# Columns turned half a chunk later, and one modulation shared by ScalarE and POOL, at the entry of the second attention layer

## The reference

```python
shift, scale, gate = jnp.split(silu_c @ w_ada[i] + b_ada[i], 3, axis=-1)
u = h * (1.0 + scale[:, None, :]) + shift[:, None, :]
uc = hc * (1.0 + scale_c) + shift_c
if i % N_MIXERS == 0:
    y, yc = mixer_a(u, uc, ...)      # windowed attention
else:
    y, yc = mixer_b(u, uc, ...)      # 2-D neighbourhood attention
h = layer_norm_2(DEEPNORM_ALPHA * h + gate[:, None, :] * y, ln_g[i], ln_b[i])
```

## Time and profile before

| | |
|---|---|
| median of three runs | 2012.42 us (2010.51 to 2013.0) |
| the profiled execution's own time | 2013.87 us |
| its span | 2012.0 us |
| TensorE busy | 1960.5 us, 97% |
| VectorE busy | 1052.8 us, 52% |
| ScalarE busy | 802.6 us, 40% |
| POOL busy | 725.9 us, 36% |
| mean granted clock of TensorE | 0.992 of 2.4 GHz |

### The profile page before, as it was taken

How to read it: one execution, slowest core, us unless ns; L and a number is a source line. 1 busy time by engine, 2 the same in 40 slices (tenths; PEclk the granted TensorE clock), 3 DMA queues, 4 the chain that set the end, 5 groups by cost and what they waited for, 6 DMA issues and landing times.

```text
span 2012.0 us, 36191 instructions
## 1 busy us (share of the span) xinstructions
PE 1960.5 (97%) x14644; PEld 1627.4 (81%) x14644; DVE 1052.8 (52%) x2196; ACT 802.6 (40%) x1568; POOL 725.9 (36%) x559
## 2 busy tenths in 40 slices
PE   7999999999999999999999999999999999999996
PEld 5888888888887888888888788778888888888785
DVE  4556655865856554556665732733333333334625
ACT  3110110110125565566767620645454454555601
POOL 3333333333345822221222524562232232232545
PEclk9999999999999999999999999999999999999998
DMA  4423322232232401100111423131111111111333
GB/s 160 136 84 95 107 93 81 98 114 74 84 105 85 154 16 36 46 22 25 35 36 35 135 79 116 53 126 43 46 40 43 49 37 43 50 35 43 111 121 136
DMA packets 51044, 152.24 MB, mean 76 GB/s; under 512 B 5440, under 2 KB 11200, under 8 KB 50752
## 3 DMA queue, kind: packets, MB, share of 16 engines
q1 hardware_dynamic: 50160, 148.73, 22.3%
q10 hardware_dynamic: 720, 1.20, 0.2%
HBM read 129.20 MB, written 20.71 MB: 75 GB/s over the span
## 4 chain that ended last, share of the span: by engine, by line
PE 65%; DVE 3%; ACT 2%; issue 2%; POOL 1%; DMA 0%; DVEq 0%; SPq 0%; POOLq 0%
PE psum L935 16%; PE psum L936 15%; PE psum L937 15%; PE psum L1123 7%; PE psum L1071 6%; PE psum L1087 5%; PE psum L944 1%; POOL w_lo L758 0%; ACT u_tmp L1335 0%; DMA w_raw<-weights_in 0%; ACT u_hi L1336 0%; DVE logits L1848 0%; ACT logits L1411 0%; DVE prob_t L1870 0%; DVE u_lo L1715 0%
## 5 line engine op out<-in xcount | busy, mean ns | idle before, releaser
L935 PE MATMUL psum<-u_hi,w_hi 128*128 128x512 f32 (+1 forms) x1440 | 545.8, 379 | 3.0 <-DVE u_lo L1715 2.1
L936 PE MATMUL psum<-u_lo,w_hi 128*128 128x512 f32 (+1 forms) x1440 | 527.3, 366 | 0.0
L937 PE MATMUL psum<-u_hi,w_lo 128*128 128x512 f32 (+1 forms) x1440 | 526.7, 366 | 0.0
L756 POOL CAST w_hi<-w_raw 128x1024 fp32r<-128x1024 f32 x140 | 152.9, 1092 | 992.6 <-DMA w_raw<-weights_in 992.6
L758 POOL TENSOR_TENSOR w_lo<-w_raw,w_hi 128x1024 fp32r<-128x1024 f32 x140 | 348.0, 2486 | 11.2
L935 PEld LDWEIGHTS psum<-u_hi,w_hi 128*128 128x128 f32 x1440 | 272.6, 189 | 57.1 <-DVE u_lo L1715 3.7
L937 PEld LDWEIGHTS psum<-u_hi,w_lo 128*128 128x128 f32 x1440 | 272.8, 189 | 46.2
L936 PEld LDWEIGHTS psum<-u_lo,w_hi 128*128 128x128 f32 x1440 | 273.1, 190 | 40.2
L1411 ACT ACTIVATE logits<-logits,neg_max 128x641 f32<-128x641 f32 (+4 forms) x272 | 214.2, 788 | 58.5 <-DVE neg_max L1848 55.5
L935 PE MATMUL psum<-x_hi,w_hi 128*128 128x512 f32 x512 | 201.3, 393 | 14.9 <-DVE x_lo L1570 13.4
L1439 ACT ACTIVATE prob_t<-psum 128x320 f32<-128x320 f32 (+1 forms) x272 | 114.5, 421 | 244.0 <-PE psum L1087 243.5
(11 more groups left out here) (171 smaller groups left out, 2910.2 us busy)
## 6 DMA issues: line engine op xcount, KB each, us to landing
w_raw<-weights_in SPq DMA_DIRECT2D x140, 512.0 KB, 3.6
w_ada<-w_ada_in SPq DMA_DIRECT2D x48, 512.0 KB, 3.5
residual<-act_buf SPq DMA_DIRECT2D x4, 2048.0 KB, 7.5
res<-residual SPq DMA_DIRECT2D x26, 256.0 KB, 3.4
y_all<-staged SPq DMA_DIRECT2D x24, 256.0 KB, 4.5
act_buf<-x_t_in SPq DMA_DIRECT2D x8, 512.0 KB, 13.8
tab<-bias_tab_in SPq DMA_DIRECT2D x16, 244.5 KB, 4.5
staged<-a_y SPq DMA_DIRECT2D x6, 640.0 KB, 3.0
```

The costliest lines, as they stand in the source:

```text
L756: pool.tensor_copy(w_hi[:, slot, :], w_raw[:, slot, :]).then_inc(w_hi_done, 1)
L935: pe.matmul(out, wh, xh, start=first, stop=False)
L936: pe.matmul(out, wh, xl, start=False, stop=False)
L937: return pe.matmul(out, wl, xh, start=False, stop=last)
```

## The change

The change has three parts, all in the entry of the second attention layer.

- TensorE turns tiles 6 to 9 back to columns half a chunk (12 matmuls) later than before, and tiles 8 and 9 to rows half a chunk later too. ScalarE's and VectorE's `take` of q0, k0 and v0 are moved to fit: ScalarE takes v0 before it stores tile 9, VectorE takes q0 before it normalises tile 8 and k0 before tile 9.
- The last half's modulation is shared. ScalarE makes only the fp32r part (`modulate_last`). POOL makes the fp32 value `u_tmp` in eight instructions after `root(1, 9)`, and waits first until all columns of the norm are stored. VectorE's `u_lo` of that chunk waits for both.
- The last half's residual scaling goes from POOL to ScalarE (`residuals_last`, after the take of v2); each of its eight instructions waits for POOL's read of the same values, and SyncE's store of that half waits for ScalarE.

```diff
@@ SyncE: store_residual
-            sp.wait_ge(res_ready, KT * (3 * layer + n + 1))
+            if (layer, n) == (1, 1):
+                sp.wait_ge(last_res, KT)
+            else:
+                sp.wait_ge(res_ready, KT * (3 * layer + n + 1))
@@ POOL
         root(1, 8)
         root(1, 9)
+        pool.wait_ge(ln_stored, LN0[2])
+        for k in range(KT):
+            n = mod_count(1, 1) - KT + k
+            pool.wait_ge(mod_split, n - MOD_SLOTS + 1)
+            pool.tensor_scalar(u_tmp[:, n % MOD_SLOTS, :], act_buf[:, k, HALF:S], par[:, 6, k:k + 1], par[:, 7, k:k + 1],
+                               ALU.mult, ALU.add).then_inc(last_u, 1)
         residuals(1, 0)
...
         first_bias(0)
-        residuals(1, 1)
         for n in range(B_UNIT, B_UNIT + 4):
             split(n + W_SLOTS)
@@ TensorE: start_b
             project(1, row, 0, 4, KT)
+            project(1, row, 1, 0, 4)
             to_columns(1, 6)
             to_rows(1, 8)
-            project(1, row, 1, 0, 4)
+            project(1, row, 1, 4, KT)
             to_columns(1, 7)
             to_rows(1, 9)
-            project(1, row, 1, 4, KT)
+            project(1, row, 2, 0, 4)
             to_columns(1, 8)
-            project(1, row, 2, 0, 4)
+            project(1, row, 2, 4, KT)
             to_columns(1, 9)
-            project(1, row, 2, 4, KT)
             rest_of_start(1, 3)
@@ ScalarE
+        def modulate_last(*ks):
+
+            for k in ks:
+                act.activation(u_hi[:, k, HALF:S], act_buf[:, k, HALF:S], ACT.Identity, scale=par[:, 6, k:k + 1],
+                               bias=par[:, 7, k:k + 1]).then_inc(mod_done, 1)
+
+        def residuals_last():
+
+            for k in range(KT):
+                act.wait_ge(last_u, k + 1)
+                x = act_buf[:, k, HALF:S]
+                act.activation(x, x, ACT.Identity, scale=par[:, 10, k:k + 1], bias=par[:, 11, k:k + 1]).then_inc(last_res, 1)
@@ ScalarE: start_b
             store_columns(1, 6)
+            take(1, row[1])
             store_columns(1, 7)
-            take(1, row[1])
             store_columns(1, 8)
+            take(1, row[2])
             store_columns(1, 9, settle=True)
-            modulate(1, 1, 0, 1)
-            take(1, row[2])
-            modulate(1, 1, 2)
+            modulate_last(0, 1, 2)
             take(1, row[3])
-            modulate(1, 1, *range(3, KT))
-            rest_of_start(1, 4)
+            modulate_last(*range(3, KT))
+            take(1, row[4])
+            residuals_last()
+            rest_of_start(1, 5)
@@ VectorE: low_part
                 dve.wait_ge(mod_done, n + 1)
+                if (layer, ch) == (1, 1):
+                    dve.wait_ge(last_u, k + 1)
@@ VectorE: start_b
             normalise(1, 7)
+            take(1, row[0])
             normalise(1, 8)
-            take(1, row[0])
             low_part(1, 2, *range(4, KT))
+            take(1, row[1])
             normalise(1, 9)
-            take(1, row[1])
-            low_part(1, 1, 0, 1, 2)
+            low_part(1, 1, 0, 1)
             take(1, row[3])
-            low_part(1, 1, *range(3, KT))
+            low_part(1, 1, *range(2, KT))
```

More of the change, by code:

```diff
@@ L458, in build @@
     mod_done, mod_split = sem("mod_done"), sem("mod_split")
+    last_u, last_res = sem("last_u"), sem("last_res")
     res_ready, res_stored = sem("res_ready"), sem("res_stored")
```

## The result

| | before | changed |
|---|---|---|
| runs, median of 6 each (lowest to highest) | 2012.71 us (2010.51 to 2016.22) | 2019.90 us (2018.43 to 2022.41) |
| profiled execution: own time; span | 2013.87; 2012.0 | 2020.12; 2018.3 |
| mean granted clock of TensorE | 0.992 | 0.991 |

The ratio is 1.0030, with a 95% interval of 1.0019 to 1.0042: the changed kernel is slower by 3.8 to 8.5 us, at best estimate 6.0. The spans of the two profiled executions differ by 6.3 us, the two medians by 7.2.

The account below looks back on a forecast made before the run. TensorE, busy 97% of the span, was taken as the bound, with POOL setting g0's start after the change. g0 +3.4 us and clock +2.0 gave +5.4 on 2012.4: 2017.8 us, range 2013.8 to 2020.2.

Parts of the forecast that it names:

- TensorE's part: Entry of second attention layer: two waits go, 0.6 us wait at tile 9 comes, k2 starts 3.1 us earlier.
- The 1.6 us of slow clock: TensorE behind the 1.71 us wait: eight matmuls at 1.2 GHz cost about 1.6 us more, which the change removes.
- the 0.9 us in q1 go too, with 1.1 us of cover: q1: POOL's pace of 0.96 us per value removes the 0.9 us loss, eighth split done 1.1 us before needed.
- POOL's sixteen scalings: POOL's u_tmp and first-half residual, beside eight VectorE splits: 15.3 us, as in the first attention layer.
- The eight u_tmp about 7.7: POOL's eight fp32 values for the last half's modulation: about 7.7 us in the profile, not 6.0.
- Tables and tiles: POOL's tables and tiles after the residual, without splits beside them: 9.0 us, done at 1329.8.
- The queue: SyncE's load of g0's weights behind the first half's store lands at 1330.2, so the cast begins then, not 1329.8.
- The clock: TensorE at g0 after 7.4 us idle: slow matmuls cost 2.0 us, ends 1.6 and 2.6.
- The part costed at nothing: ScalarE swaps eight fp32 values for eight later residual scalings of the same size: no cost.
- Faster: g0's weights ready by 1326.4, at a POOL chain of 21.0 us: TensorE keeps 4.0 us, 2008.4 us; chance 0.06.
- Light contention: VectorE and POOL, in step, may not hinder each other: g0 +0.2, clock +2.0, 2014.6 us; chance 0.15.
- The load held by the second store: Second 2 MB store delays g0's load 1.5 to 7.2 us, taken as 5: +10.4, 2022.8 us; chance 0.07.

Follow-up runs that it names:

- weights first, mixed: Changed kernel with g0's weights loaded before the residual stores and split before POOL's tables, ScalarE making the fp32 values of tiles 3 and 6; 2008.82 us, ratio 0.9977.
- weights first: Changed kernel with g0's weights loaded before both residual stores and split by POOL before the bias tables and tiles; 2010.07 us, ratio 0.9981.
- mixed: Changed kernel with first half's residual in POOL's earlier pauses, g0's load before stores, split after first-build tiles, ScalarE making values 3 and 6; 2010.91 us, ratio 0.9983.
- residual early: Changed kernel with the first half's residual moved into POOL's pauses ahead of the roots of tiles 7 and 9; 2011.07 us, ratio 0.9990.
- small splits: Changed kernel with VectorE's eight splits of the last half covering 8 columns instead of 512; 2015.13 us, ratio 1.0006.
- load first: Changed kernel with only SyncE's order altered: the load of g0's weights ahead of both residual stores; 2020.09 us (one run).
- kept busy: Changed kernel with 26 matmuls ahead of g0 whose product is not used; 2017.80 us, ratio 1.0016.
- sharing only: Changed kernel with the turning and the takes as before, only the modulation shared; 2020.91 us, ratio 1.0027.
- before, weights first: Kernel before with g0's weights loaded ahead of the stores and split ahead of the last half's residual; 2019.18 us, ratio 1.0030.

## Why the prediction was right, and where it was off

The direction, the mechanism and nearly the size were right: +5.4 us forecast, +6.3 in the spans, 6.5 by the count from T and 7.2 in the medians of six runs. The changed kernel's median, 2019.9, lies in the range near its upper end. Of times said on the clock of the kernel before, 0.36 us of the difference is T, which came that much later in the changed profile. By the prediction's own steps:

- **TensorE's part.** Right. Said: a wait of 0.6 us ahead of tile 9, k2 3.1 us earlier, q1 at 1310.1. Measured: 0.70, 3.17 (from T), 1310.46. The terms given for VectorE add up to 1303.4, not to 1303.6. The 1.6 us of slow clock are a price of the one profile read: the last kernel of the table has the same wait and did not pay it.
- **"the 0.9 us in q1 go too, with 1.1 us of cover".** Wrong. q1 took 6.63 us (1310.46 to 1317.09), more than the 6.34 before. The step took 0.96 us per value from the other layer's average over sixteen scalings, but the eight that have a subtraction beside each go in step with it at 1.20 to 1.27 us. The eighth u_tmp ended at 1315.4, not at 1313.1 (2.0 us late from T). It cost nothing here, since TensorE waits for g0 afterwards anyway: it was ready at 1328.1, not at 1326.4, and idled 6.7 us, not 7.4. It does cost where g0 doesn't wait: with six values on POOL, weights first, mixed starts g0 1.3 us before weights first, and mixed 1.6 us before residual early. In small splits q1 was at full rate too, but g0 waited for POOL all the same.
- **POOL's sixteen scalings**, said 15.3: 16.1 (9.59 + 6.55). Small splits give 0.5 us for each subtraction, where the rows of the other layer gave 0.4 (15.3 less 12.1, by eight). "The eight u_tmp about 7.7" was the mis-sized half: 9.59. This 0.8 us is the shortfall at g0, which came 4.06 us late (from T) against 3.4; the tables and tiles gave 0.2 of it back.
- **Tables and tiles**, said 9.0: 8.8 (1322.05 to 1330.85). Right.
- **The queue.** Said: the load lands 9.4 us after the store's issue, 0.4 behind POOL. Measured: 9.26 and 0.39. Right as a price, and load first shows how little hangs on it: 0.26 us at g0, as POOL is behind it anyway.
- **The clock**, said 2.0 with ends at 1.6 and 2.6: 2.46, and 2.4 by the kernel that was kept busy. Nearer to the upper end.
- **The part costed at nothing**, eight residual scalings on ScalarE: right. ScalarE did them from 1311.97 to 1317.72. Its take of q1 began 0.5 us after k1's start and not 0.2, and TensorE did not wait for it.

The rivals: *Faster* needed a POOL chain of 21.0 us from the last columns. It was 28.9 (1305.85 to 1334.71). With the weights first it took 19.7 (1303.50 to 1323.20), which meets this rival's condition, and that kernel is faster than the kernel before, by 2.7 us from T where the rival said 4.0. *Light contention* fell: the two engines do go in step, as it supposed, but being in step makes it dearer, 4.0 us over eight. *The load held by the second store* fell: the load landed 8.8 us after its issue though the second store went out 0.6 us behind it. (The least delay that the rival reckoned with, 1.5 us, is 1.8 by its own rule, 0.5 MB at 2.5 MB per 9.0 us.) What I left out as a rival is an order of POOL's program that keeps the change's gain; I took the order as given.

Open: why the clock cost 2.46 us in the changed kernel, and 1.49 and 1.57 (7.26 and 7.34 from g0 to the scores, less 5.77) with the load first and with small splits, after idles of 6.3 and 3.9 us. Idle length alone doesn't order them, for sharing only, after 5.3 us, paid 2.5; and ahead of it, after the same 1.7 us wait, the kernel before paid 1.6 us while before, weights first paid nothing. No run here isolates the reason.

## What to carry to other kernels

When work moves onto an engine that runs its program in order, follow that engine's queue to the next thing that the bounding engine needs, not only to the work moved. Here eight cheap scalings that waited for the last columns pushed a weight's split, due 20 us later, behind that wait, and cost 7.1 us, more than the 3 us that TensorE had won by the other half of the change. The cure was not to undo it but to put what is due ahead of what is not, once nothing that has a deadline stood behind it. And two engines in lock-step over shared operands need a price measured in lock-step: an average over a longer stretch was too low here (0.96 us per scaling, against 1.20).

## What the runs showed of the hardware

- A POOL scaling of 128x512 fp32 took 0.76 us alone. With one of VectorE's two-input subtractions of the same size beside each, it took 1.20 us, and the pair ran at one per 1.27 us. That is 0.5 us of POOL's time per subtraction (4.0 over eight, small splits), and it works the other way too: with four POOL scalings near them, four VectorE subtractions of 128x256 from SBUF took 1.92 us, not 1.43, while its statistics and scaling from PSUM took no longer (residual early). Twice that made tile 9 0.98 us late.
- The price of a low clock after a pause was not a fixed one: 1.5 to 2.5 us after pauses of 3.9 to 6.7 us, paid as seven (load first, small splits) to some twelve (changed, sharing only) matmuls that start 0.43 us apart instead of 0.23. 26 unused matmuls in the pause kept it at 1.00. After the same wait of 1.7 us, followed by the same turns, the clock was 0.50 in one profile (before) and 1.00 in another (before, weights first).
- A 512 KB load issued 0.4 us behind a 2 MB store landed 8.8 us after its issue, in the changed kernel and again with small splits (1319.00 to 1327.82). With a 2 MB store issued 0.4 us behind it and none ahead (before, weights first), it landed after 5.0 us; with none issued within 4 us on either side, after 3.4 and 4.5 us (load first, weights first).
